# Projections, attention, gate and output of a mixer put into one interleaved order (one Trainium2 core)

## The reference

```python
q_x, k_x, v_x, gu_x, gv_x = split(hx @ w_in)      # 1024, 1024, 1024, 512, 512 columns
q_x, k_x = rope(q_x), rope(k_x)                   # 8 heads, two maps of 64 each
k_c, v_c = split(hc @ w_in[:, QK_W:2*QK_W+V_W])   # context: keys and values only
k_all, v_all = concat(k_c, k_x), concat(v_c, v_x) # 512 keys
s = einsum('qhmd,khmd->hmqk', q_x, k_all) / 8
p = softmax(s)
a = p[:, 0] - lam * p[:, 1]                       # differential attention
o = einsum('hqk,khe->qhe', a, v_all)              # 128 columns for each head
a_x = o * rsqrt(mean(o * o) + eps) * g * 0.8      # head norm
v = layer_norm(gelu(gv_x)); u = gelu(gu_x)
g_x = u * (einsum('gpq,qgc->pgc', w_s, v) + b_s)  # spatial gate, 4 groups of 128 columns
y_x = concat(a_x, g_x) @ w_out                    # 1536 -> 1024
```

## Time and profile before

| | |
|---|---|
| median of 3 runs | 2224.16 us (2223.94 to 2224.31) |
| the profiled execution, its own time | 2223.49 us |
| its span in the trace | 2221.7 us |
| busy in the span | PE 1822.1, PEld 1095.4, DVE 1471.4, ACT 877.2, POOL 622.3 us |
| DMA | 723.76 MB, mean 326 GB/s |
| mean granted clock of TensorE | 0.937 of full speed |

### The profile page before, as it was taken

One profiled execution on the slowest core, in us unless ns is written; L12 is line 12 of the kernel. 1 busy time (PEld: TensorE's weight loads), 2 busy tenths in 40 slices (PEclk: granted clock), 3 DMA queues, 4 the chain that ended last, 5 costly groups with the idle time before them and its releaser, 6 DMA issues.

```text
span 2221.7 us, 21883 instructions
## 1 busy us (share of the span) xinstructions
PE 1822.1 (82%) x7101; PEld 1095.4 (49%) x7101; DVE 1471.4 (66%) x3020; ACT 877.2 (39%) x2284; POOL 622.3 (28%) x567
## 2 busy tenths in 40 slices
PE   4887999899877688888877877996888788877886
PEld 3757998799756443434322332354444343322332
DVE  6767956855676657667667677525576777677755
ACT  3445433523343234334434444312343444444433
POOL 1160000000000333534353443203344344444441
PEclk7889989898988799999999999998999999999999
DMA  9653758546334499999999999944999999999996
GB/s 370 261 195 124 263 203 303 210 178 259 114 133 143 188 384 411 420 418 421 394 406 421 422 421 421 367 170 195 371 405 420 419 421 421 421 421 421 421 422 252
DMA packets 114690, 723.76 MB, mean 326 GB/s; under 512 B 11504, under 2 KB 13344, under 8 KB 34064
## 3 DMA queue, kind: packets, MB, share of 16 engines
q0 software_dynamic: 74864, 540.30, 58.8%
q1 hardware_dynamic: 39712, 182.07, 22.1%
HBM read 721.24 MB, written 1.08 MB: 325 GB/s over the span
## 4 chain that ended last, share of the span: by engine, by line
PE 40%; DMA 31%; DVE 19%; ACT 4%; issue 4%; POOL 1%; SPq 0%; DVEq 0%; ACTq 0%; POOLq 0%
DMA X<-in_k_uv,EI 16%; PE PS L1980 14%; DMA Z<-in_k_uv,EI 7%; DMA W<-in_peer_wq 5%; PE PS L1957 5%; PE PS L1672 4%; PE PS L1674 4%; PE PS L1673 4%; DVE junk L1659 4%; DVE ACC L1273 3%; DMA W<-in_ada_w 2%; DVE WL L1289 2%; PE PS L1760 2%; PE PS L2033 1%; PE PS L1995 1%
## 5 line engine op out<-in xcount | busy, mean ns | idle before, releaser
L1980 PE MATMUL PS<-X,dg 128*128 128x512 f32 x1372 | 666.4, 620 | 170.2 <-ACT dg L911 167.6
L1659 DVE CUSTOM_DVE_ANT_0 junk<-H,X 128x1024 f32<-128x1024 f32 x343 | 420.0, 1225 | 244.4 <-DMA X<-in_k_uv,EI 237.6
L902 POOL DMA_INDIRECT X<-in_k_uv,EI x343 | 376.7, 1098 | 620.8 <-PE PS L1980 360.3
L1980 PEld LDWEIGHTS PS<-X,dg 128*128 128x128 f32 x1372 | 247.1, 193 | 544.2 <-ACT dg L911 337.8
L911 ACT ACTIVATE CF<-DOT 128x1 f32<-128x1 f32 x512 | 102.2, 200 | 581.9 <-DVE DOT L1659 578.6
L1980 PE MATMUL PS<-Z,dg 128*128 128x512 f32 x504 | 248.8, 628 | 51.7 <-ACT dg L911 51.0
L911 ACT ACTIVATE dg<-CP,CG 128x128 f32<-128x128 f32 x512 | 205.5, 401 | 16.9
L1659 DVE CUSTOM_DVE_ANT_0 junk<-H,Z 128x1024 f32<-128x1024 f32 x126 | 154.3, 1225 | 86.9 <-DMA Z<-in_k_uv,EI 80.9
L1980 PEld LDWEIGHTS PS<-Z,dg 128*128 128x128 f32 x504 | 93.4, 197 | 190.4 <-ACT dg L911 111.1
L902 POOL DMA_INDIRECT Z<-in_k_uv,EI x126 | 138.5, 1099 | 140.9 <-PE PS L1980 120.0
L1672 PE MATMUL PS<-XH,WH 128*128 128x256 f32 x592 | 173.3, 293 | 4.2 <-DVE WL L1289 2.3
(11 more groups left out here) (294 smaller groups left out, 2636.7 us busy)
## 6 DMA issues: line engine op xcount, KB each, us to landing
W<-in_ada_w SPq DMA_DIRECT2D x51, 1024.0 KB, 6.2
Y<-in_ada_w SPq DMA_DIRECT2D x21, 1024.0 KB, 5.7
W<-in_peer_wq SPq DMA_DIRECT2D x16, 1024.0 KB
W<-in_k_ffi SPq DMA_DIRECT2D x13, 1024.0 KB, 6.0
Y<-in_k_ffi SPq DMA_DIRECT2D x9, 1024.0 KB, 4.9
Y<-in_k_win SPq DMA_DIRECT2D x9, 1024.0 KB, 8.3
W<-in_ffn_w_out SPq DMA_DIRECT2D x8, 1024.0 KB, 5.3
W<-in_k_win SPq DMA_DIRECT2D x7, 1024.0 KB, 6.9
```

The source lines that it names most:

```text
L902: e.indirect_dma_start(out=WS[k][:, :], out_offset=None, in_=I[f"k_uv{ly}"][:, :], in_offset=bass.IndirectOffsetOnAxis(ap=EI[t][:, j:j + 1 ...
L1659: e.tensor_tensor_reduce(junk, H[:, t, :], d[:, 0:D], 1.0, 0.0, ALU.mult, ALU.add, DOT[:, j:j + 1]).then_inc(v_dot, 1)
L1980: p = e.matmul(PS[:, 2 * t + q, :], dgb[n % 4][:, :], d[:, D + q * 512:D + (q + 1) * 512], start=(j == 0), stop=(j == 127))
```

## The change

The mixer is put into one interleaved order. The projection parts come by pairs of heads (queries, keys, values of pair 0, then of pair 1, and so on; `WIN_ORDER`), and the units go by head, both token halves of one head after another. The first 20 quarters (pair 0) run with the context's transposes. Then each unit is five or six slots, and in each slot one quarter of a generator `fillers` is issued behind a step of the attention: the rest of the projections, then the first five output parts. `ring3` moves ahead of all projections, as the attention's buffers E and AT now lie where two of the five ring buffers and the rows R2 to R5 are. Scores have one pair of banks instead of two; each unit's output goes from bank 3 to a buffer OB and its squares are summed by ACT; `hs` and `hs2` norm four units at a time; `turn_head` transposes a head at a time into the halves K2r, over the keys of heads that are done. Row 5 moves into `between(0)`, rows 3 and 4 behind the last unit, and the loads of R5 and R1 wait for `p_do` 16 and `p_row` 10. The modulation product 9 moves behind the last output part. Of a part with context and token halves, each half has its own bank and eviction (`evac`, `evc`).

```diff
-WIN_ORDER = list(range(8)) + [14, 15, 12, 13] + list(range(8, 12))
+WIN_ORDER = [0, 4, 8, 1, 5, 9, 14, 2, 6, 10, 15, 3, 7, 11, 12, 13]
+AO_ORDER = [0, 1, 4, 5, 2, 3]
...
+    P("ring3")
+    P("ldctx")
+    P("ldlam")
     for c in range(8):
-        xt(2, c, bank(low))
-    P("ldctx")
-    P("lam")
+        xt(2, c, 4 + c % 4)
     split(IN + 1)
...
+    def products():
+
+        group, rope, pend = 0, 0, None
+        for i in range(16):
+            n, tile = IN + i, WIN_ORDER[i]
+            for q in range(quarters(n)):
+                b = 6 + group % 2
+                P("gq", n, q, b)
+                if q in (2, 5) and pend is not None:
+                    P("rope2", *pend)
+                    pend = None
+                if q == 3:
+                    P("evac", n, b, rope)
+                    if tile < 8:
+                        pend = (rope, tile)
+                        rope += 1
+                    group += 1
+                elif q == 7:
+                    P("evc", n, b)
+                    group += 1
+                if q == quarters(n) - 1:
+                    P("ldw", n + 2)
+                    split(n + 2)
+                yield
+
+    steps = iter(range(43, 72))
+    mods = {47: 6, 55: 7, 63: 8}
+    due = []
+
+    def step(b):
+        while due:
+            mod(due.pop(), b)
+        m = next(steps, None)
+        if m is not None:
+            ada(m)
+            if m in mods:
+                due.append(mods[m])
+
+    def turn_head(h, b):
+        P("xp", 4, h, b)
+        P("xt", 4, h, b)
+        P("xl", 4, h)
+
+    def part(i):
+        n = AO + i
+        for q in range(4):
+            P("gq", n, q)
+            yield
+            if q == 3 and i < 4:
+                P("ldw", n + 2)
+                split(n + 2)
+
+    def fillers():
+        yield from products()
+        for i in range(5):
+            yield from part(i)
+
+    g = fillers()
+    for k in range(20):
+        if k < 8:
+            xt(3, k, k % 4)
+        if k == 8:
+            P("lam")
+            P("gn8")
+        if k % 5 == 4:
+            step(5)
+        next(g)
+
+    norms = {9: 0, 10: 1, 11: 2, 12: 3}
+    gates = {(13, 0): 0, (13, 4): 1, (14, 2): 2, (14, 4): 3}
+    for n in range(16):
+        for k in range(6):
+            if k == 0 and n:
+                P("dt", n - 1)
+                if n >= 4 and n % 4 == 1:
+                    P("hs2", n // 4 - 1)
+            elif k == 1:
+                P("ds", n)
+            elif k == 3 and n:
+                P("do", n - 1)
+                if n % 4 == 0:
+                    P("hs", n // 4 - 1)
+            elif k == 4:
+                P("dn", n)
+            elif k == 5:
+                if n >= 4 and n % 4 in (1, 2):
+                    turn_head(2 * (n // 4 - 1) + n % 4 - 1, 4 if n < 13 else 3)
+                if n in norms:
+                    P("gn", norms[n])
+            if k == 2 or k == 5 and n % 2:
+                step(5 if n < 13 else 2)
+            if n in (6, 7, 8) and k == 2:
+                row(2, n - 6, 5)
+            if (n, k) in gates:
+                P("gate", gates[n, k], 2)
+            if k < 5 or n >= 4:
+                next(g)
+    P("dt", 15)
+    next(g)
+    step(0)
+    P("do", 15)
+    P("hs", 3)
+    next(g)
+    P("rowv", 3)
+    row(3, 1, 0)
+    next(g)
+    row(3, 2, 1)
+    P("hs2", 3)
+    P("rowv", 4)
+    next(g)
+    turn_head(6, 2)
+    row(4, 1, 0)
+    turn_head(7, 3)
+    row(4, 2, 1)
     P("fold", 0)
     P("sc", 0)
...
+    for _ in part(5):
+        pass
+    P("modp", 9, 0)
...
-            for w in (6, 7, 8):
+            for w in (5, 6, 7, 8):
                 yield from rowsteps(w, 3)
...
-                        for s, n in y_free:
-                            w.wait_ge(s, n)
-                        w.wait_ge(p_row, 12)
+                        w.wait_ge(p_do, 16)
+                        w.wait_ge(p_row, 10)
...
+                    w.wait_ge(p_mod, 10)
                     e.indirect_dma_start(out=WS[k][:, :], out_offset=None, in_=I[f"k_uv{ly}"][:, :],
...
+                elif kind == "do":
+                    n = a[0]
+                    w.wait_ge(p_do, n + 1)
+                    if n >= 8:
+                        w.wait_ge(p_xt, nth("xp", 4, 2 * (n // 4) - 3))
                     else:
-                        w.wait_ge(a_gsq, 2)
-                    act(junk, PS[:, 6:8, :].rearrange("p a b -> p (a b)"), ACT.Square).then_inc(a_hsq, 1)
-                    sqrt_of(st[:, 48 + 8 * t:56 + 8 * t], nth.rs["hn", t])
+                        w.wait_ge(a_sq, 4)
+                    act(OB[n // 4 % 2][:, n % 4, :], PS[:, 3, 0:128], ACT.Copy)
+                    if n:
+                        w.wait_ge(a_ob, n)
+                    o = 48 + n % 8
+                    act(DOT[:, :], PS[:, 3, 0:128], ACT.Square, accum_out=st[:, o:o + 1]).then_inc(a_ob, 1)
```

More of the change, by code:

```diff
@@ L260, in make_plan @@
+    P("dt", 15)
[15 more added lines that the diff above has]
+    row(4, 2, 1)
     P("fold", 0)
     P("sc", 0)
[L262 to L272, removed]
+    for _ in g:
+        pass
@@ L498, in __init__ @@
                 if not (FI <= n < FO and (n - FI) % 2):
-                    ev += 2 if len(a) > 1 and a[2] is not None else 1
+                    ev += 1
                 self.ev[n] = ev
                 if n >= IN and WIN_ORDER[n - IN] < 8:
-                    self.rope_part[a[3]] = n
-            if kind in ("rms", "hn", "rn", "brn", "frn") or name == ("gn", 1):
+                    self.rope_part[a[2]] = n
+            if kind == "evc":
+                ev += 1
+                self.evc[a[0]] = ev
+                self.dual[a[0]] = count[kind]
+            if kind in ("xt", "gate"):
+                uses += 1
+                self.use[name] = uses
+                if kind == "xt":
+                    halves[a[1] % 2] += 1
+                    self.turned_by[name] = halves[a[1] % 2]
+            if kind in ("xl", "gate"):
+                lows += 1
+                assert self.use[("xt", *a) if kind == "xl" else name] == lows
+            if kind in ("rms", "hs", "rn", "brn", "frn") or name == ("gn", 1):
                 rs += 1
@@ L531, in __init__ @@
         w = {t: IN + i for i, t in enumerate(WIN_ORDER)}
-        self.ev_k, self.ev_g, self.ev_u, self.ev_v = (max(self.ev[w[t]] for t in ts) for ts in (
-            range(4, 8), (14, 15), (12, 13), range(8, 12)))
+        self.ev_g, self.ev_u = self.ev[w[15]], [self.ev[w[12]], self.ev[w[13]]]
+        self.keys, self.values = [self.evc[w[4 + p]] for p in range(4)], [self.evc[w[8 + p]] for p in range(4)]
     def __call__(self, *name):
@@ L672, in build @@
         units = [(s2, i, t) for s2 in range(2) for i in range(4) for t in range(2)]
-        order = [(t, hd) for t in range(2) for hd in range(8)]
+        order = [(t, hd) for hd in range(8) for t in range(2)]
         d_cp, d_x, d_sm, d_sm2, d_tab, d_sk, d_td, d_be = (sem("d_" + n) for n in (
@@ L1002, in _ @@
                         w.wait_ge(v_add, 4)
-                        if x == "k":
-                            h = 2 * (tile - 4)
-                            act(K2[:, h:h + 2, 0:256], two(a[2]), ACT.Copy).then_inc(a_ev, 1)
                         if x in "qk":
-                            i = a[3]
+                            i = a[2]
                             if i >= 2:
@@ L1020, in _ @@
                             act(gv[:, :, z], two(b), ACT.Gelu_apprx_tanh).then_inc(a_ev, 1)
+                elif kind == "evc":
+                    n, b = a
+                    tile = WIN_ORDER[n - IN]
+                    w.wait_ge(p_part, n + 1)
+                    if tile < 8:
+                        h = 2 * (tile - 4)
+                        act(K2[:, h:h + 2, 0:256], two(b), ACT.Copy).then_inc(a_ev, 1)
+                    else:
+                        z = slice((tile - 8) * 256, (tile - 7) * 256)
+                        act(V2[:, 0:2, z], two(b), ACT.Copy).then_inc(a_ev, 1)
                 elif kind == "as":
@@ L1452, in _ @@
                     n = a[0]
-                    t, hd = order[n]
                     z = st[:, 24 + 8 * (n % 3):32 + 8 * (n % 3)]
@@ L1716, in out_part @@
                     k, t = t, k
-                kk = 2 * i + k
-                xh, xl = x(kk, t)
+                xh, xl = x(2 * r + k, t)
+                first, last = 2 * i + k == 0, 2 * i + k == nk - 1
                 split_half(n, k)
```

236 lines of the change are left out of this document (125 added, 111 removed), and 2 rows, old and new, of tables (d_gath, p_x).

## The result

The changed kernel takes 2241.76 us (median, 2238.84 to 2246.86) beside 2224.05 us of the kernel before on the same chip: ratio 1.0087, 95% interval 1.0064 to 1.011. It is slower: the medians are 17.7 us apart, and the ratio over all runs of the two says 0.87%. 2229 was predicted. Measured a second time, beside the last experiments, the ratio was 1.0099 (1.0084 to 1.0114). The profiled execution took 2241.01 us, its span is 2239.2.

The account below looks back on a forecast made before the run. TensorE was taken to bound the projections and VectorE the attention; 419.2 + 232.1 + 43.8 + 4.8 + 15.7 + 10.4 put the addition at 726.0, 3.1 us gained, then 7.8 lost behind it: 2229 us, range 2197 to 2250.

Parts of the forecast that it names:

- Waits of PE in the units: In the attention units TensorE waits, mostly for the normalisation queued behind a weight part's split: 43.8 us, bounds 16 and 58.
- The tail: Behind unit 15: 4.8 us of wait before the row vectors, then 10.4 from last row product to addition, through R1's load.
- The clock: Half-clock spells in the mixer, at first projections, three modulation products and nine waits over 3 us: 15.7 us, bounds 5 and 35.
- 232.1: TensorE's own work in the mixer up to the last row product, moved together with no wait: 232.1 us.
- ScalarE's tables: In the mixer, table loads rise from 7 to about 15 at 1.28 us each, already counted in the waits.
- the rival that charged them twice: Rival: a table switch costs twice its row, seven in the chains, 9.0 us more: 2238 us, chance 0.04.
- Behind the stage: Beside the experts, row 5's five added steps delay expert 128's indices (EI): 7.8 us later, bounds 3 and 10.
- The ring of three: Three weight buffers instead of five in the mixer: loads stay hidden, no cost; without that cover 30 us in all.
- The clock falls more often: Rival: the attention stage's clock of 0.82 throughout the mixer, 35 us more, some 22 replacing waits: 2242 us, chance 0.14.
- The overlap holds: Rival: 22 us of waits and 4 of spells in the mixer, 2203 us; faster once waits are under 39; chance 0.34.

Follow-up runs that it names:

- experiment 1: Changed kernel with each unit's normalisation issued ahead of the weight part's split halves where a part ends in slots 1 to 3: 2206.36 us, ratio 0.9932.
- experiment 2: Changed kernel with the normalisation issued ahead of the split halves in slot 3 alone: 2218.70 us, ratio 0.9992.
- Experiment 5: Changed kernel with rows 3 and 4 spread into the rotations' buffers, so that R1's row is loaded early: 2237.85 us, ratio 1.008.
- Experiment 3: Changed kernel with useless matmuls filling six of TensorE's waits: 74 of them 2237.42 us, ratio 1.0067; 48, cut to the waits' length, 2228.81 us, ratio 1.0031.
- experiment 7: Changed kernel with u and the gate's values copied instead of applying Gelu in the mixer: 2241.02 us, ratio 1.0089.
- experiment 6: Changed kernel with row 5's steps in one turn beside the experts: 2234.71 us, ratio 1.0053; rows 5 to 8 in four turns: 2239.96 us, ratio 1.0088.

## Why the prediction was right, and where its sum was not

The direction was right, the time 12.8 us too low, inside the range. Two slips in its additions cancel: 16 units of 0.9, 1.0 and 0.5 are 38.4 and not 37.6, and by its own figures units 13 and 15 have 2.0 and 2.8 of wait, not 3.3 and 2.3. Its steps in order:

- **Waits of PE in the units, 43.8.** Right in sum and in most places, and its mechanism is shown by experiments 1 and 2. Predicted and measured: unit 0 4.0 and 3.77; unit 2 3.9 + 0.8 and 4.70; unit 4 4.8 + 2.4 and 6.28; unit 6 2.3 and 2.11; units 8 and 12 4.8 each and 4.26 each; unit 13 3.3 and 2.87, with 1.5 and 0.79 at its gate. Too high: unit 10 4.6 and 2.12, unit 14 5.6 and nothing, unit 15 2.3 and 0.36. Two costs that it didn't have made up for these: the head transposes in the rotations' bank, 3.88 and 3.89, where it had 1.4 in units 5 and 9 for another reason, and 2.64 in two waits for the context's low halves (at 436.51 and 439.56). The sum was right partly because errors of both signs cancelled.
- **The tail.** 4.8 predicted, 4.39 measured. From the last row product to the addition 10.4 predicted, 10.5 measured (730.3 to 740.83), with R1's row awaited for 5.54. Experiment 5 shows that it is this load.
- **The clock, 15.7: the term that was mis-sized.** The last row product ended at 730.3, predicted 715.6. Start 420.0 instead of 419.2 is 0.8; the waits give back 1.1. That leaves 310.3 - 232.1 - 47.5 = 30.7 where 15.7 stood, 15.0 over; 0.8 - 1.1 + 15.0 are the 14.7 us. Not all of the 30.7 is the clock. Of the 61 us at half clock some 10 lie inside the waits and cost nothing; in the other 51 TensorE worked, with a projection matmul every 0.21 us (480.10 to 480.32) instead of 0.12, which makes 22 us lost, and half of them, 26, is the most it can be. The other 5 to 8 us are work that the 232.1 lacked. The trace shows a place for most of it: the first projection matmul behind an attention step takes 0.20 us to the next one at full clock (640.71 to 640.91), not 0.12, and over 60 such changes of step are some 5 us, an estimate. A unit's own steps were priced about right (at full clock scores 1.06, products 0.81, transposes 0.35 to 0.41; charged 0.9, 1.0 and 0.5).

  Experiment 3 shows that filling six of the waits takes some 22 us off the half clock and, by ratios, 15 off the time. The prediction charged 8.6 us for nine waits, about one each; of the waits shown above, those of 6.28 and 4.26 have 6.8 us at half clock each. It also charged 2.0 for the first projections, which ran at full clock here, and 1.7 for each of three modulation products, of which two had such stretches away from any wait (3.4 and 6.8 us). The bounds of 5 and 35 held the term. The rows already had the better estimate: clocks of 0.94 and 0.87 over two stretches of 166 and 93 us are 20 + 24 us at half clock, half of which is 22, before the third stage is counted. The Trainium skill, "TensorE: Matmul & The Clock Gate", section "HAM oscillation", which the prediction cites, says of waits for data between short bursts that they bring the clock back each time; by it the prediction had an estimated 2248. These waits are for VectorE, and the trace agrees in kind, for ten of the eleven waits over 2 us, though not for the one of 2.11 at 568.15. The time came out nearer to 2248 (6.2 below) than to 2229 (12.8 above).
- **ScalarE's tables.** Once their row, in the waits, shown by experiment 7 for three waits; the rival that charged them twice falls. The Trainium skill, "ScalarE: Activation LUTs", section "What ACT_TABLE_LOAD costs", has a drain of about 1380 ns with each switch; 1.4 us of wait for a load of 1.28 leaves no place for it here.
- **Behind the stage, 7.8.** 5.8 measured in the span, EI 5.1 later. That it is the turns is shown by experiment 6 and by the table: with row 5 in one turn the part behind the addition returns to 1491.4 to 1493.4, before's 1492.6. The size was 2 us too high; the bounds of 3 and 10 held it. The path was wider than forecast: the lag isn't only in front of expert 128 but grows over the next heads. Experiment 7 has 1492.8 there too, with its turns unchanged and no edit there, so a single execution's figure is good to some 5 us only, and the claim rests on experiment 6's time as well.
- **The ring of three, at no cost.** Agreed: in the mixer ACT waits 1.2 us for a weight part, once, and DVE not at all for the modulation's loads (6.2 us over the whole span).
- **The account.** +4.7 us predicted for the span, +17.5 measured: -3.1 became +11.8 (14.7 later than forecast at the last row product, by the clock and by work that was not counted, and 0.1 in the tail), and +7.8 became +5.8.
- **The rivals.** "The clock falls more often", 2242 us, is what came nearest, with 0.14. Its time is met, but partly by luck: it had 35 us more of clock than charged, with 22 of them in place of waits, and the runs show 7 to 10 more, with the waits as long as forecast. "The overlap holds" needed waits under 39 us in the units; with the tail's 4.39 taken off there were 43.1. Experiment 1 made it come true by the order of two steps.

## What to carry to other kernels

Where an engine's queue is in order, look at each step that waits for a late producer and ask what ready work stands behind it; moving 0.8 us of ready work ahead of such a wait was worth 34 us here. When waits are put into a dense TensorE stage, price them with the clock behind them: take the granted clock of the stretches that have such waits now, and charge 0.4 to 0.5 of the time at half clock in which TensorE works (22 to 26 of 51 us here). Compare the waits of the order before and after: an interleaving that only moves them gains nothing. A chain of small steps that alternates between two engines needs other work between its steps, but each step it is spread over delays what follows: test both ends.

## What the runs showed of the hardware

Useless matmuls in the waits made the kernel faster: 48 of them, 21 us of TensorE's time in waits, gave back some 15 us by ratios, with the granted clock of 520 to 540 us at 1.00 instead of 0.83. The clock also stood at half behind work: around a modulation product of 32 matmuls with one column each (4.45 us at 643.67) the 6.8 us from 646.3 were at 0.50 with no wait near. Eight matmuls of 128x128 by 128x128 took 1.05 us at the full clock and 2.07 at half in the row products of experiment 6, where TensorE worked for 2 us and waited for 0.7 to 1.7 by turns.
